# Second norm with stored and kept row tiles in turn, and the gate z multiplied in at the chunk attention

## What is computed

```python
h = rmsnorm(x, norm_g)                                   # the "second norm"
proj = h @ w_in
q, k, v, z_att, gb, gc, u, z_conv, g_att, g_conv = split(proj)
att = chunked_rel_attention(q, k, v, rel_bias)           # 8 heads of 64, 9 chunks of 64 keys
y_att = (att * silu(z_att)) @ w_att_out
y_conv = (gb * causal_conv(gc * u) * silu(z_conv)) @ w_conv_out
m = sigmoid(g_att) * y_att + sigmoid(g_conv) * y_conv
x = x + m @ w_out
return rmsnorm(x, final_norm_g)
```

## Time and profile before

| | us |
|---|---|
| median of 3 timed runs | 3469.47 |
| lowest and highest of them | 3466.7, 3471.64 |
| the profiled execution's own time | 3459.93 |
| its span, first to last instruction | 3458.1 |
| TensorE busy in it | 3087.2 (89%) |
| VectorE, ScalarE, GpSimd busy | 1822.1, 1275.9, 670.3 |
| mean granted TensorE clock | 0.939 of full |

### The profile page before, as it was taken

How to read it: one execution, slowest core, us unless ns; L and a number is a source line. 1 busy time by engine, 2 the same in 40 slices (tenths; PEclk the granted TensorE clock), 3 DMA queues, 4 the chain that set the end, 5 groups by cost and what they waited for, 6 DMA issues and landing times. The chain is left out here.

```text
span 3458.1 us, 61901 instructions
## 1 busy us (share of the span) xinstructions
PE 3087.2 (89%) x23542; PEld 2567.2 (74%) x23542; DVE 1822.1 (53%) x3200; ACT 1275.9 (37%) x2646; POOL 670.3 (19%) x567
## 2 busy tenths in 40 slices
PE   5997998796999988969729999999999889959799
PEld 5886997686999985648627888878888656648687
DVE  5555442163555545655355577575676355543333
ACT  4222433153444437831132323343323267720132
POOL 0000000142333320023153232242323111120000
PEclk8998999897999998979959999999999989979899
DMA  3221774252343324046453322353223350064543
GB/s 129 73 73 70 249 233 142 86 153 97 131 131 128 131 98 137 24 139 203 150 158 110 103 66 83 117 180 105 86 67 110 114 150 17 17 223 153 198 145 116
DMA packets 293977, 423.26 MB, mean 122 GB/s; under 512 B 41713, under 2 KB 185073, under 8 KB 288497
## 3 DMA queue, kind: packets, MB, share of 16 engines
q1 hardware_dynamic: 251600, 383.88, 33.2%
q10 hardware_dynamic: 42144, 36.18, 3.3%
HBM read 270.56 MB, written 149.42 MB: 121 GB/s over the span
## 5 line engine op out<-in xcount | busy, mean ns | idle before, releaser
L106 PE MATMUL pj_pp<-h_hi,pj_whi 128*128 128x512 f32 x1344 | 525.6, 391 | 31.9 <-DVE pj_wlo L2792 27.1
L107 PE MATMUL pj_pp<-h_lo,pj_whi 128*128 128x512 f32 x1344 | 524.4, 390 | 0.0
L108 PE MATMUL pj_pp<-h_hi,pj_wlo 128*128 128x512 f32 x1344 | 524.2, 390 | 0.0
L106 PEld LDWEIGHTS pj_pp<-h_hi,pj_whi 128*128 128x128 f32 x1344 | 253.1, 188 | 86.5 <-issue 34.0
L108 PEld LDWEIGHTS pj_pp<-h_hi,pj_wlo 128*128 128x128 f32 x1344 | 253.2, 188 | 52.9
L107 PEld LDWEIGHTS pj_pp<-h_lo,pj_whi 128*128 128x128 f32 x1344 | 253.3, 188 | 52.0
L2729 ACT CAST pj_whi<-w_raw 128x512 fp32r<-128x512 f32 x240 | 149.0, 622 | 337.6 <-PE pj_pp L108 314.2
L2792 DVE TENSOR_TENSOR pj_wlo<-w_raw,pj_whi 128x512 fp32r<-128x512 f32 x240 | 229.3, 956 | 80.7 <-ACT pj_whi L2729 77.8
L106 PE MATMUL pc_pp<-h_hi,pc_whi 128*128 128x512 f32 x384 | 150.7, 393 | 9.9 <-DVE pc_wlo L346 9.9
L2920 POOL TENSOR_TENSOR w_raw<-w_raw,pj_t 128x512 f32<-128x512 f32 x48 | 62.6, 1305 | 454.6 <-DVE pj_wlo L2792 454.6
L107 PE MATMUL pc_pp<-h_lo,pc_whi 128*128 128x512 f32 x384 | 150.5, 392 | 0.0
(11 more groups left out here) (343 smaller groups left out, 7332.1 us busy)
## 6 DMA issues: line engine op xcount, KB each, us to landing
w_raw<-in_w_second SPq DMA_DIRECT2D x192, 256.0 KB, 2.7
ds_pk<-scratch_pack SPq DMA_DIRECT2D x32, 1280.0 KB, 7.5
scratch_pack<-rp_out SPq DMA_DIRECT2D x32, 512.0 KB, 2.7
scratch_sig_fm<-pj_ob SPq DMA_DIRECT2D x64, 256.0 KB, 2.1
mb_sg<-scratch_sig_fm SPq DMA_DIRECT2D x16, 1024.0 KB, 6.9
rp_fm<-scratch_qkv_fm SPq DMA_DIRECT2D x96, 128.0 KB, 2.8
scratch_qkv_fm<-pc_acc SPq DMA_DIRECT2D x11, 1024.0 KB, 4.8
n_x<-in_x SPq DMA_DIRECT2D x16, 512.0 KB, 4.3
```

The source lines that it names most:

```text
L106: nc.tensor.matmul(out, ah, bh, start=(first and i == 0), stop=False)
L107: nc.tensor.matmul(out, ah, bl, start=False, stop=False)
L108: mm = nc.tensor.matmul(out, al, bh, start=False, stop=(last and i == n - 1))
```

## The change

In norm_combine stored and kept pairs alternate: even pairs are stored, odd ones kept. The rounding and the remainders of a kept pair n-1 are issued in every stored pair's turn, and VectorE takes the remainder of MID from GpSimd. In attention an optional gate_fm is loaded, one 256 KB piece a tile on ScalarE's queue, and VectorE multiplies it into each half of ob. chunk_attention passes z_fm. merge_branches loads no z and GpSimd does nothing there; the second tile's weights are loaded ahead of the first sigmoid gate instead of behind it.

```diff
@@ attention
+        gb = [c.sb(f"gb{s}", [P, PAIRS, P]) for s in S] if gate_fm is not None else None
+        half_gated = c.sem("half_gated")
+        gate_in = c.sems("gate_in", 2)
@@ finish, VectorE
                 nc.vector.tensor_tensor(ob[s][:, 2 * half:2 * half + 2, :], o_ps[half][:, 0:2, :], rd[half][:],
                                         ALU.mult).then_inc(half_done[half], 1)
-                if half:
+                if gb is not None:
+                    pair = slice(2 * half, 2 * half + 2)
+                    dve.wait_ge(gate_in[s], 16 * u + 16 + START)
+                    dve.wait_ge(half_done[half], t + 1 + START)
+                    ins = nc.vector.tensor_tensor(ob[s][:, pair, :], ob[s][:, pair, :], gb[s][:, pair, :], ALU.mult)
+                    ins.then_inc(normed[s] if half else half_gated, 1)
+                elif half:
                     dve.wait_ge(half_done[half], t + 1 + START)
                     dve.sem_inc(normed[s], 1)
@@ tile, ScalarE
                         exponent(now, m, g)
+                        if m == 0 and g == 0 and gb is not None:
+                            t, u, s = now[0:3]
+                            act.dma_start(gb[s][:], gate_fm[:, :, bass.ds(t * P, P)].rearrange("m p t -> p m t")).then_inc(
+                                gate_in[s], 16)
@@ norm_combine
+        STORED, KEPT = range(2)
         def tile(n, e):
-            return (TILES // 2) * (1 - n // 4) + 4 * e + n % 4
+            return (TILES // 2) * (1 - n % 2) + 4 * e + n // 2
         def place(n):
-            return slice((n % 4) * P, (n % 4 + 1) * P)
+            return slice((n // 2) * P, (n // 2 + 1) * P)
@@ SyncE
-                if n < DIRECT:
+                if n % 2 == STORED:
@@ ScalarE
-                if 2 <= n < DIRECT + 2:
-                    act.wait_ge(stored[s], 16 * N_COMB * u + START)
-                elif n >= DIRECT + 2:
-                    act.wait_ge(top_lo[s], u - DIRECT // 2 + START)
+                if s == STORED:
+                    act.wait_ge(stored, 16 * N_COMB * u + START)
+                else:
+                    act.wait_ge(top_lo, u + START)
...
-                if n > DIRECT:
+                if n > 0 and s == STORED:
                     round_hi(n - 1)
@@ VectorE
                 nc.vector.tensor_tensor(clo[:, LOW, :, at], cb[s][:, LOW], chi[:, LOW, :, at].bitcast(F32),
-                                        ALU.subtract).then_inc(low_lo[s], 1)
+                                        ALU.subtract).then_inc(low_lo, 1)
+                dve.wait_ge(mid_hi, u + 1 + START)
+                nc.vector.tensor_tensor(clo[:, MID, :, at], cb[s][:, MID], chi[:, MID, :, at].bitcast(F32),
+                                        ALU.subtract).then_inc(mid_lo, 1)
...
-                if n > DIRECT:
+                if n > 0 and s == STORED:
                     low_rest(n - 1)
@@ GpSimd
-                pool.wait_ge(mid_hi[s], u + 1 + START)
-                nc.gpsimd.tensor_tensor(clo[:, MID, :, at], cb[s][:, MID], chi[:, MID, :, at].bitcast(F32),
-                                        ALU.subtract).then_inc(mid_lo[s], 1)
-                if n >= DIRECT + 2:
-                    pool.wait_ge(mid_lo[s], u - DIRECT // 2 + START)
+                if s == KEPT:
+                    pool.wait_ge(mid_lo, u + START)
...
-                if n > DIRECT:
+                if n > 0 and s == STORED:
                     rest(n - 1)
@@ merge_branches, SyncE
+            def next_w(i):
+                sp.wait_ge(w_lo, i + 1 + START)
+                sp.wait_ge(c_lo, GROUPS + START)
+                load_w(sp, i + 1)
+
             def step(i, more):
-                if more:
-                    sp.wait_ge(w_lo, i + 1 + START)
-                    sp.wait_ge(c_lo, GROUPS + START)
-                    load_w(sp, i + 1)
                 sp.wait_ge(m_done, i + 1 + START)
...
-                sp.dma_start(ahi[:, :, cols[g]].bitcast(F32), z_fm[:, :, cols[g]].rearrange("m p t -> p m t")).then_inc(
-                    a_in[g], 16)
+            next_w(0)
             sp.wait_ge(a_lo, GROUPS + START)
             load_sig(sp, 0)
-            with sp.Fori(0, KT - 1) as i:
+            step(0, True)
+            with sp.Fori(1, KT - 1) as i:
+                next_w(i)
                 step(i, True)
-        @block.gpsimd
-        def _(pool):
-            for g in G:
-                pool.wait_ge(a_in[g], 32 + START)
-                nc.gpsimd.tensor_tensor(az[g], az[g], ahi[:, :, cols[g]].bitcast(F32), ALU.mult).then_inc(gated, 1)
@@ merge_branches, ScalarE
-                act.wait_ge(gated, g + 1 + START)
+                act.wait_ge(a_in[g], 16 + START)
@@ chunk_attention
-              (lambda m: m, lambda m, g: HD * (2 * m + g)), (4, 4, 512), (5, TILES - 1, 0), out)
+              (lambda m: m, lambda m, g: HD * (2 * m + g)), (4, 4, 512), (5, TILES - 1, 0), out,
+              gate_fm=z_fm)
```

More of the change, by code:

```diff
@@ L1752, in attention @@
 def attention(nc, name, consts, load_tile, n_kt, bias_of, bias_shape, load_bias, sink_rows, lanes, shapes, span, out,
-              ahead_load=None):
+              ahead_load=None, gate_fm=None):
     key_tile, value_at = lanes
@@ L2343, in norm_combine @@
         s4_ready = c.sems("s4_ready", 2)
[L2344 to L2350, removed]
+        top_hi = c.sem("top_hi")
+        low_hi = c.sem("low_hi")
+        mid_hi = c.sem("mid_hi")
+        low_lo = c.sem("low_lo")
+        top_lo = c.sem("top_lo")
+        mid_lo = c.sem("mid_lo")
+        stored = c.sem("stored")
         w_ahead = c.sem("w_ahead")
@@ L2353, in norm_combine @@
         TOP, LOW, MID = slice(A11, A12 + 1), slice(A22, S3 + 1), slice(S2, S4 + 1)
-        DIRECT = PAIRS // 2
+        STORED, KEPT = range(2)
         def tile(n, e):
-            return (TILES // 2) * (1 - n // 4) + 4 * e + n % 4
+            return (TILES // 2) * (1 - n % 2) + 4 * e + n // 2
         def place(n):
-            return slice((n % 4) * P, (n % 4 + 1) * P)
+            return slice((n // 2) * P, (n // 2 + 1) * P)
         @block.sync
@@ L2383, in _ @@
                     for a in range(N_COMB):
-                        sp.dma_start(later[a, :, :, place(n)], cb[s][:, a]).then_inc(stored[s], 16)
+                        sp.dma_start(later[a, :, :, place(n)], cb[s][:, a]).then_inc(stored, 16)
             for r in S:
@@ L2387, in _ @@
                     sp.dma_start(w_raw[r][q], w_first[q][:, r * K4W:(r + 1) * K4W, :]).then_inc(w_ahead, 16)
-            for s in S:
-                sp.wait_ge(stored[s], 16 * N_COMB * DIRECT // 2 + START)
+            sp.wait_ge(stored, 16 * N_COMB * PAIRS // 2 + START)
             sp.wait_ge(w_ahead, 64 + START)
@@ L2405, in round_hi @@
             def round_hi(n):
-                s, u, at = n % 2, n // 2 - DIRECT // 2, place(n)
+                s, at = n % 2, place(n)
                 act.wait_ge(top_ready[s], n // 2 + 1 + START)
-                nc.scalar.copy(chi[:, TOP, :, at], cb[s][:, TOP]).then_inc(top_hi[s], 1)
+                nc.scalar.copy(chi[:, TOP, :, at], cb[s][:, TOP]).then_inc(top_hi, 1)
                 act.wait_ge(low_ready[s], n // 2 + 1 + START)
-                nc.scalar.copy(chi[:, LOW, :, at], cb[s][:, LOW]).then_inc(low_hi[s], 1)
+                nc.scalar.copy(chi[:, LOW, :, at], cb[s][:, LOW]).then_inc(low_hi, 1)
                 act.wait_ge(s4_ready[s], n // 2 + 1 + START)
-                nc.scalar.copy(chi[:, MID, :, at], cb[s][:, MID]).then_inc(mid_hi[s], 1)
+                nc.scalar.copy(chi[:, MID, :, at], cb[s][:, MID]).then_inc(mid_hi, 1)
             roots(0)
@@ L2445, in low_rest @@
             def low_rest(n):
-                s, u, at = n % 2, n // 2 - DIRECT // 2, place(n)
-                dve.wait_ge(low_hi[s], u + 1 + START)
+                s, u, at = n % 2, n // 2, place(n)
+                dve.wait_ge(low_hi, u + 1 + START)
                 nc.vector.tensor_tensor(clo[:, LOW, :, at], cb[s][:, LOW], chi[:, LOW, :, at].bitcast(F32),
-                                        ALU.subtract).then_inc(low_lo[s], 1)
+                                        ALU.subtract).then_inc(low_lo, 1)
+                dve.wait_ge(mid_hi, u + 1 + START)
+                nc.vector.tensor_tensor(clo[:, MID, :, at], cb[s][:, MID], chi[:, MID, :, at].bitcast(F32),
+                                        ALU.subtract).then_inc(mid_lo, 1)
             dve.wait_ge(w_in, 16 + START)
@@ L2458, in _ @@
                 dve.wait_ge(turned[2 * s + 1], u + 1 + START)
[L2459 to L2462, removed]
+                if s == STORED:
+                    dve.wait_ge(stored, 16 * N_COMB * u + START)
+                else:
+                    dve.wait_ge(low_lo, u + START)
                     dve.wait_ge(s4_ready[s], u + START)
@@ L2476, in rest @@
             def rest(n):
-                s, u, at = n % 2, n // 2 - DIRECT // 2, place(n)
-                pool.wait_ge(top_hi[s], u + 1 + START)
+                s, u, at = n % 2, n // 2, place(n)
```

(15 more changed lines are left out.)

## The result

Before: 3463.19 us, median of 8 executions (3449.03 to 3476.2). After: **3433.29 us**, median of 8 (3421.98 to 3450.42). The ratio is 0.991, 95% interval 0.9888 to 0.9933: 31 us faster, between 23 and 39. The profiled execution of after took 3436.93 us, its span 3435.2.

The account below looks back on a forecast made before the run. TensorE, busy 89% of the span, was taken as the bound, with time lost where it stands. Norm -3.9, attention +4.7 and merge -24.2 summed to -23.4 us: 3469.47 to 3446, range 3436 to 3458.

Parts of the forecast that it names:

- eight subtractions, 2.2 us apart: Merge: without z, VectorE's subtractions run unslowed, the last ending at 3063.8 instead of 3085.0.
- The gate product: Merge: VectorE's product waits for the sigmoid load, issued at 3063.85 and landing in 7.9 us, at 3071.7.
- The half clock: Merge's start: TensorE granted 1.2 GHz, some ten matmuls 0.43 us apart, 0.2 us each lost.
- Rival (a): Merge gains half, -13, bound by landings and half clock; total -12, time 3457 us; chance 0.13.
- The turns: Norm: two pairs share a turn of stores, load arrival and engine work, 21.4 us together.
- The engines' chain: Norm's tail: last copies, cast and remainders on VectorE and GpSimd, ending about 1808, 3 us either way.
- four weight loads 2.95 us, then 7.1 us to land: Norm's tail on SyncE: after pair 6's stores end at 1800.8, weights land at 1810.9, the later end.
- the forecast's own second chain: Norm's tail on the engines, ending about 1808, earlier than SyncE's 1810.9.
- The term 0.34 a tile: Chunk attention: half 1's new multiply delays the key copy and TensorE; 12 x 0.34 = 4.1 us.
- (c): Attention pays for everything, 22 us over 15 tiles; total -6, about no change; chance 0.05.
- (d): Attention: half 1's multiply waits for GpSimd's copy of values, 32 us in all; time 3478 us; chance 0.02.
- Rival (b): Norm gains nothing or loses, +4 in place of -3.9; total -15.5, time 3454 us; chance 0.17.

Follow-up runs that it names:

- k2: The kernel before with z loaded in the merge but GpSimd's multiply left out, so its output lacks z; merge 218.5 us in one execution.
- k3: The changed kernel with the norm of before; 3449.13 against 3467.13 us, ratio 0.9943.
- h1: The kernel before with the changed norm alone; 3459.01 against 3463.66 us, ratio 0.998.
- h2: The changed kernel with the remainder of MID given back to GpSimd, alternation kept; norm 105.6 us in one execution.
- g2: The changed kernel, unchanged, as a further sample; 3436.35 us, ratio 0.9919 to the kernel before.
- g3: The changed kernel once more, unchanged; 3438.86 us, ratio 0.9915 to the kernel before.
- g4: The changed kernel with the norm's load of pair n+3 issued ahead of pair n's stores; 3428.18 us, ratio 0.989, norm 89.5 us.
- k4: The changed kernel with norm loads and the norm's last weight loads ahead of stores, and the last key copy ahead of the finish; 3416.9 us, ratio 0.9861.
- g1: The kernel before, run unchanged as a further sample; ratio 0.9986 to the kernel before.

## Where the forecast held, and where it failed

The table column by column, after against before:

- **Merge, forecast -24.2, measured -24.2** (mean of three executions of after). The step "eight subtractions, 2.2 us apart" put the last end at 3063.8; it came at 3064.11. The gate product was put at 3071.7 and started at 3071.61. The half clock was there as forecast: products start 0.43 us apart up to 3050.31, 14 of them where I took ten, so the 96 products took 24.9 us in place of 24.2 and the wait behind them was 4.52, not 5 to 6. That the product came within 0.1 us is in part luck: the sigmoid was issued 0.3 later than forecast, and its 7.9 us to landing, which no row shows (it is the median over all loads into that buffer), was 7.5. Rival (a), a merge that gains only half, would have shown 217 us; k2 with 218.5, which has the loads of z but not the multiply, is what that looks like.
- **Norm, forecast -3.9, measured -7.6**, near the end of my bounds (-8 to +4). The turns were right (21.4 against 22). The last stores start 88.6 us after the last addition, where the working put S4 of pair 6 at 88.3. The engines' chain was right as well: VectorE's last remainder ends at 1811.29 + 3.35 = 1814.64, 100.6 us after the addition, forecast 101 (1808 - 1707.0). **The step that failed is "four weight loads 2.95 us, then 7.1 us to land".** The 7.1 comes from the earlier trace rows, where these loads were issued behind the loads of a pair and had to share with them. There four loads of 512 KB were issued in the 2.6 us ahead of them. At the end of the new order the seven stores of 256 KB are ahead of them, issued over 5.5 us, and they land in 4.0. The old norm in k3 again gives 7.0 to 7.2, and the loads of h1, h2, g2, g3, g4 and k4 take 3.7 to 5.0; no run changes what is ahead of them and nothing else. SyncE's end is then 3.1 us earlier, level with the engines', and the forecast's own second chain gives the time. k4 and g4 fit: with the weights out of the way, half a microsecond was to be had.
- **Attention, forecast +4.7, measured +1.3 to +3.6**. The term 0.34 a tile was mis-sized: it is 0.19. I added the multiply's whole step to a distance of 0.68 us, but 0.15 of that went with the edit: from the finish it was 0.68 to the copy, through a wait for VectorE's own result (the drain wait) and the increment of the semaphore normed as an instruction of its own; now it is 0.53 to the multiply, which carries the increment. I had written that the drain wait "exists already" and did not price the instruction that the diff deletes beside it. That the removed increment is what the 0.15 was, I infer from the two rows; no run has it alone. The ten tiles give 1.9 us in place of 3.4. The three tiles ahead of them, from the fourth to the tenth finish of a half, take 47.2 us where before they took 46.3, 0.9 more, and the end behind the last finish 16.4 to 16.6 where it was 15.9 and 16.0, about 0.5 more (forecast 0.6). So the gate itself costs about 3.3 us, not 4.7. The rest of the scatter lies between the first and the fourth finish: 21.6 and 22.1 us in before and g1; 19.5, 21.6 and 22.0 in the three executions of after. There the clock is granted at half for longer or shorter: over the 30 us from the first score the mean granted clock is 0.74 in after (19.5 us), 0.62 and 0.61 in the other four.
- **Rivals (c) and (d)** are out. In (c) half 0's multiply, drain and loads would be paid: the tiles show 0.19 us. In (d) a multiply that met GpSimd's copy of values would be longer or start later; the 32 lie within 3 ns of each other, and the ten tiles leave room for 0.19 us each. Rival (b), a norm that gains nothing or loses, is out by h1.

The Trainium skill (SBUF — State Buffer, Who interferes with whom) has VectorE with two SBUF inputs and GpSimd exclude each other. The norm's tail in after agrees in the sum: from 1809.48 to 1814.64 VectorE's LOW and MID and GpSimd's TOP take 5.2 us, and one by one they would take 1.88 + 1.23 + 2.33 = 5.4; MID alone takes 3.35 there. In h2, where MID is GpSimd's, the stretch is only about a microsecond longer: here two engines that take turns gained little from sharing.

Summed up with the forecast's terms replaced by the measured ones: -7.6 + 2.6 - 24.2 = -29.2, against -23.4; the gap and the last projection, at -0.9 and +0.5, had no term. The forecast of 3446 was then 12.7 us above the measured 3433.29: half of that (6.3) is the base, since the three runs shown had a median of 3469.47 and later ones 3463.19 to 3467.13, and half (6.5) is the size of the gain. The low end of the range took all three best bounds at once from that higher base, and had nothing in it for the base's own scatter of some 6 us. So the range was missed through three terms: the landing of the weights, the price of the multiply, and a base from three runs.

The profiled execution of after, 3436.93 us, lies 0.4 from the 3436.5 that the sum gave for a profiled execution. That is chance: it gained more than forecast in the stretches and lost 7 to 9 us in the scan, which the change does not touch.

## What to carry to other kernels

A landing time belongs to its place in the queue: before using a row's "issue to landing", look at what was issued ahead of it, there and in the new order. Price what a diff deletes beside an instruction (here, as far as the rows tell, an increment), not only what it adds. And where the same queue carries stores that wait for an engine and loads that engines wait for, put the loads first: that edit took 15 us off the norm's stretch here (10 by the timing, 5 to 14), where the new order of the pairs took off 7.6.

## What the runs showed of the hardware

- The same 256 KB weight loads took 7.1 us to land behind four loads of 512 KB and 4.0 behind seven stores of 256 KB (after).
- One stage, the same in all fourteen traces, came to its last product between 1286.0 and 1308.5 us, with a granted clock of 0.93 to 0.85 within 800 to 1050. One profile's span can't show a change of 10 us; the stretches of norm and merge repeated within 1.1 us.
- With the same subtractions, GpSimd's four multiplies of 128x2048 beside VectorE cost the merge 11.3 us (before against k2), more than the loads of 4 MB did (8.5, k2 against k1).
- Issued behind seven stores that wait for engines, the loads of the norm made a turn 22 us long; issued ahead of them, 15 and 18 (g4).
